# GpSimd's weight sums of two gate chunks, held behind two results of VectorE

## What is computed

```python
h = rms_norm(x); proj = h @ w_in            # q/k/v of both branches, beta, decay, gates
y_a = diff_attention(dq, dk, dv)            # 4 heads, two softmaxes each: p0 - lam*p1
y_b = gated_delta_net(...) * silu(g_gate)   # 4 chunks of 64 tokens, solved by inverses
merged = sigmoid(m_gate_a) * (y_a @ w_branch_attn) + sigmoid(m_gate_b) * (y_b @ w_branch_gdn)
x = x + merged @ w_out
x = x + hier_moe(rms_norm(x))               # 32 experts, top 2 of one group
return rms_norm(x)
```

## Time and profile before

| | us |
|---|---|
| median of 3 runs | 458.78 (458.12 to 460.59) |
| the profiled execution, its own time | 460.23 |
| its span, first to last instruction | 458.5 |
| PE busy | 427.2 (93%) |
| DVE busy | 223.8 (49%) |
| ACT busy | 124.3 (27%) |
| POOL busy | 60.2 (13%), 94 instructions |
| mean granted clock of PE | 0.970 |
| moved by DMA | 136.92 MB, 299 GB/s on average |

### The profile page before, as it was taken

How to read it: one execution, slowest core, us unless ns; L and a number is a source line. 1 busy time by engine, 2 the same in 40 slices (tenths; PEclk the granted TensorE clock), 3 DMA queues, 4 the chain that set the end, 5 groups by cost and what they waited for, 6 DMA issues and landing times.

```text
span 458.5 us, 10749 instructions
## 1 busy us (share of the span) xinstructions
PE 427.2 (93%) x4503; PEld 340.8 (74%) x4503; DVE 223.8 (49%) x573; ACT 124.3 (27%) x326; POOL 60.2 (13%) x94
## 2 busy tenths in 40 slices
PE   8999999999997999999999899999999987779784
PEld 7885598884896999988888778677686755537451
DVE  3376777996366388513322655343444522432233
ACT  5001522100500163610012533233242312222144
POOL 4010600000693449000000000000000000000001
PEclk9999999999997999999999999999999988998798
DMA  8969726325704053298996999999999999999992
GB/s 306 410 231 326 268 80 221 101 86 151 264 10 175 1 184 124 68 400 338 414 415 260 325 409 425 416 419 422 422 422 421 420 422 422 420 422 422 422 380 101
DMA packets 38197, 136.92 MB, mean 299 GB/s; under 512 B 8592, under 2 KB 9936, under 8 KB 26256
## 3 DMA queue, kind: packets, MB, share of 16 engines
q1 hardware_dynamic: 33808, 135.22, 74.7%
q10 hardware_dynamic: 4352, 1.21, 1.2%
HBM read 134.59 MB, written 1.84 MB: 298 GB/s over the span
## 4 chain that ended last, share of the span: by engine, by line
PE 74%; DMA 18%; DVE 3%; SPq 1%; ACT 1%; issue 1%; POOLq 0%; ACTq 0%; DVEq 0%
PE ps L996 21%; DMA arena<-in_moe_w_up 11%; PE ps L1447 10%; PE ps L1042 10%; PE ps L1311 6%; PE ps L1295 6%; DMA ring<-in_moe_w_up 6%; PE ps L1500 3%; PE ps L1490 3%; PE ps L1406 2%; PE ps L1455 1%; PE ps L1057 1%; SPq L437 1%; DMA cst_in<-in_norm_ffn_gain 1%; PE ps L1395 1%
## 5 line engine op out<-in xcount | busy, mean ns | idle before, releaser
L996 PE MATMUL ps<-arena 128*128 128x256 f32 (+1 forms) x384 | 98.6, 416 | 0.0
L996 PEld LDWEIGHTS ps<-arena 128*128 128x128 f32 x384 | 72.2, 190 | 22.3 <-issue 14.2
L1447 PE MATMUL ps<-arena 128*32 128x128 f32 x1040 | 40.5, 296 | 9.5 <-DMA arena<-in_moe_w_up 8.9
L1447 PEld LDWEIGHTS ps<-arena 128*32 128x32 f32 x1040 | 31.3, 115 | 16.1 <-DMA arena<-in_moe_w_up 7.7
L793 ACT ACTIVATE gains<-ps 32x256 f32<-32x256 f32 x62 | 23.3, 377 | 55.9 <-PE ps L1490 55.5
L559 POOL TENSOR_SCALAR ring<-ring,small 128x512 f32<-128x512 f32 x1 | 1.6, 1567 | 268.1 <-DVE small L2148 268.1
L2194 DVE TENSOR_TENSOR masks<-ps,masks 128x64 f32<-128x64 f32 x32 | 7.2, 224 | 54.8 <-ACT masks L774 54.6
L542 POOL TENSOR_TENSOR ring<-arena 128x256 f32<-128x256 f32 x32 | 22.9, 748 | 82.0 <-DMA arena<-in_w_in 70.8
L2210 DVE COPY arena<-ps 32x256 f32<-32x256 f32 x62 | 25.8, 416 | 11.2 <-PE ps L1490 10.2
L1447 PE MATMUL ps<-ring,arena 128*32 128x128 f32 x768 | 26.9, 278 | 3.6 <-DMA ring<-in_moe_w_up 3.4
L1311 PE MATMUL ps<-arena 128*128 128x256 f32 x128 | 29.3, 383 | 0.0
(11 more groups left out here) (323 smaller groups left out, 596.4 us busy)
## 6 DMA issues: line engine op xcount, KB each, us to landing
arena<-in_moe_w_down SPq DMA_DIRECT2D x19, 1024.0 KB, 26.4
arena<-in_w_in SPq DMA_DIRECT2D x8, 2048.0 KB, 8.5
arena<-in_moe_w_gate SPq DMA_DIRECT2D x16, 1024.0 KB, 22.4
arena<-in_moe_w_up SPq DMA_DIRECT2D x16, 1024.0 KB, 23.6
ring<-in_moe_w_gate SPq DMA_DIRECT2D x12, 1024.0 KB, 19.6
ring<-in_moe_w_up SPq DMA_DIRECT2D x12, 1024.0 KB, 20.5
ring<-in_moe_w_down SPq DMA_DIRECT2D x12, 1024.0 KB, 21.6
arena<-in_w_out SPq DMA_DIRECT2D x2, 2048.0 KB, 10.3
```

The source lines that it names most:

```text
L996: last = pe.matmul(out, lhs, rhs, start=(k == 0 and (i > 0 or part % 2 == 0)), stop=(k == KD - 1), skip_group_check=(i == 0))
L1447: last = pe.matmul(c.ps[ROWS * q:ROWS * (q + 1), i % 2, 0:P], c.Hg[:, k, ROWS * i:ROWS * (i + 1)], w[:, :, start:start + 127:2], start=(k ...
```

## The change

Two waits are added to GpSimd's program. In chunk `ma1` it waits for `aT_in` (the first call of `combine` done) before the first of the four forms, so all sixteen sums come behind it. In chunk `mb1` it waits for `yb_ready` before the third form, so the last eight sums (S4 and S3) come behind it. Nothing else changes: no instruction is added to another engine and none is moved within its engine.

```diff
         free("P5")
+        if name == "ma1":
+            pool.wait_ge(s["aT_in"], 1)
         combine("S1", w["A21"], w["A22"], ALU.add)
         pool.wait_ge(s["forms_combined"], combined(name, "S1"))
         free("P6")
         combine("S2", form["S1"], w["A11"], ALU.subtract)
         pool.wait_ge(s["forms_combined"], combined(name, "S2"))
         free("P3")
+        if name == "mb1":
+            pool.wait_ge(s["yb_ready"], 1)
         combine("S4", w["A12"], form["S2"], ALU.subtract)
         free("P7")
         combine("S3", w["A11"], w["A21"], ALU.subtract)
```

## The result

| | before | changed |
|---|---|---|
| median of 4 runs, us | 458.54 (458.12 to 460.59) | 454.18 (452.95 to 454.64) |
| profiled execution, its own time | 460.23 | 452.95 |
| its span | 458.5 | 451.2 |
| mean granted clock of PE | 0.970 | 0.983 |

The ratio is 0.9891 with a 95% interval of 0.9862 to 0.992: 4.4 us less by the medians, 7.3 us less between the two profiled executions. The forecast was 452.7, in a range of 451.2 to 455.8.

What follows compares the result with a forecast made beforehand. TensorE bounds the stretch from 110 to 230 us, weights the experts. Terms: -3.35 (wait) - 3.04 (clock) + 0.3 (L1910) = -6.1 us, giving 454.1 against the profiled 460.23, 452.7 against the median; range 451.2 to 455.8.

Steps and rivals of the forecast that it cites:

- the first rival: Clock falls anyway in the stretch behind the first turning, so only the wait is saved: 455.7 us; chance 5%.
- What bounds the kernel, and how a gain carries: Weights pace the experts; TensorE sets the stream's start, so its gain before 240 us moves the end by as much.
- The sums slow `combine`: GpSimd's sums in `ma1` slow VectorE's first `combine`; without them it ends at 137.34, not 141.45.
- The wait goes, 3.35 us: PE's wait before L1199, the first probabilities' transposes, vanishes; start moves from 141.60 to 138.25, a gain of 3.35 us.
- The clock, 3.04 us: From L1199 to L1208, PE's clock stays at 1.00: 4.04 us in place of 7.08, a gain of 3.04.
- bounds of 5.8 and 6.5 us: The gain's own limits: 5.8 with L1910 at 0.52 and TensorE's last matmul drained at 138.4; 6.5 with L1910 free.
- The 0.3 us at L1248: A PE wait before L1248, released by ScalarE; expected to be 0.3 to 0.9 us in the changed trace.
- L1910, 0.3 us: VectorE's small scaling ending the second query block's maxima may meet a sum: cost 0 to 0.52 us, taken as 0.3.
- Second hold, nothing: The hold in `mb1` saves 3 us of VectorE's time at L2042's eight multiplies, none of the kernel's.
- Second right sides beside sums: VectorE's `second_right_sides` (L1966), newly beside sums, costs 0 to 1.9 us extra, hidden by over 2 us of slack.
- That sums don't matter: Rival: another cause makes `combine` long, or the hold doesn't keep sums out; no gain, 458.8 to 459.1 us; chance 4%.
- GpSimd as the bound: Rival: delayed sums make TensorE wait at P6 and P7 of `ma1`, clock falling again for 3.0: 461.4 us; chance 3%.

Runs made afterwards that it cites:

- e1: The changed kernel with only the hold in `ma1`, none in `mb1`: 454.63 us, ratio 0.9903 to the kernel before.
- e4: The changed kernel plus 16 sums without use ahead of the hold in `ma1`, beside the first `combine`: 459.38 us, ratio 1.0005 to the kernel before.
- e7: The kernel before plus 13 matmuls without use ahead of the first turning of probabilities: 457.93 us, ratio 0.9961 to the kernel before.
- e3: The kernel before plus 27 matmuls without use ahead of the first turning of probabilities: 460.46 us, ratio 1.003 to the kernel before.
- after_again: The changed kernel run once more, unaltered, for a narrower interval and a second trace: 454.87 us, ratio 0.991 to the kernel before.
- e2: The changed kernel with only the hold in `mb1`, none in `ma1`: 459.91 us, ratio 1.0016 to the kernel before.
- e5: The changed kernel plus 14 memsets without use ahead of the hold in `ma1`: 456.39 us, ratio 0.9939 to the kernel before.
- e6: The changed kernel plus 8 sums without use behind the hold in `ma1`, ahead of the real ones: 458.01 us, ratio 0.9968 to the kernel before.

## Why the prediction was right, and where its size was off

The mechanism was right in both of its parts, and the forecast gain of 6.1 us was too large by a quarter or more. That the median still fell into the range is in part luck. The lower end of the gain was set by the first rival, a clock that falls in any case, and not by a stall that varies, and the median of 454.18 lies as far from the forecast (452.7) as from that rival (455.7). The number alone doesn't tell the two apart; the traces do.

**What bounds the kernel, and how a gain carries: right.** The weight stream moved with TensorE: 6.4 us at L1212 (6.9 with what lay before the mark) and 6.7 at the stream's last loads.

**The sums slow `combine`: right, shown** by e1 (with the first hold, whole gain) and e4 (idle sums in the same place, no gain). The end of `combine` was worked out as 137.34. The four scalings took 0.87 against a bound of 1.14, so it came at 136.7, on a trace that began 0.5 us earlier. At L1212 the trace read gives 6.4 us, which is 3.35 + 3.04 with nothing paid at L1910.

**The wait goes, 3.35 us: right for the trace read, too large on average.** Its row is one draw: five traces with sums beside `combine` had 3.19, 2.05, 3.15, 1.97 and 3.20 us, a mean of 2.7 (2.6 with the 2.01 of e4).

**The clock, 3.04 us: this term was mis-sized.** The mechanism holds, as the fill of e7 shows: idle time ahead, the clock falls; none, it stays. But the prediction took one execution's loss for the kernel's. Measured from the turning to L1208, over the 4.0 us at full clock, the loss was 3.1 us in the trace of before, 0.6, 3.0 and 2.2 in the three extra ones and 1.7 with only the second hold, a mean of 2.1; the 0.3 us wait at L1229 is within the 0.6 and the 2.2. The fill of e7 gained 1.5 to 1.8, with the fill's own cost taken off. The stretch as a whole gave 31.38 - 26.40 = 5.0 us on average (4.6 with the trace of e4 as a sixth). e3 gives the same by another way: its fill outlasts the stall whether that is 2.0 or 3.2 us, so from mark to L1211 it takes 148.27 - 115.85 = 32.42 us, and its median lay 1.0 above the kernel before, which puts that at 31.4 by this estimate. The prediction had noted that the profiled execution lay 1.45 us above the median and still moved the full 6.1 us over to the median. A stall that varies is likely to be above its mean in a slow execution; 6.1 less 1.45 would have been 4.7, a sum that is easy to make afterwards. It isn't the whole of the scatter, though: of the three extra traces the one with the least loss was the fastest (457.26 us), but the middle one was as slow (460.25) as the largest (460.14). The medians differ by 4.4, 4.6 and 4.8 us (the last with the first hold alone). The interval of after_again reaches from 2.9 to 5.4 us, so these runs can't tell them from 5.0. The falls of the clock in the routing, which both traces of the changed kernel have and the four of the kernel before don't, are not the change's doing alone: e2 and e7, without the first hold, have them (a mean clock of 0.93 and 0.91 from 240 to 260 us), and e1, with it, doesn't. What they cost stays open.

**Small slips in its sums.** The prediction's bounds of 5.8 and 6.5 us come out at 5.7 (3.2 + 3.04 - 0.52) and 6.4 (3.35 + 3.04). The 0.3 us at L1248 is a wait of the weight loads, not of PE, whose only wait there was the 3.2 us.

**L1910, 0.3 us: not paid, but the danger was real.** The sums of `mb0` ended at 153.74 and L1914 started at 153.60, yet took 0.17. Three runs pushed the sums later: in e5 and e6 it took 0.70 and 0.71, and PE stood 0.7 us behind it; in e4 its two instructions took 0.19 and 0.56, and PE stood 0.2 us. The term's upper bound, 0.52, was right (0.71 - 0.17 = 0.54). In the changed kernel the two rows even overlap by 0.14 us, and GpSimd's spans are rough, so by how much the place is clear isn't shown.

**Second hold, nothing: right** (e2: 1.0016, interval 0.9997 to 1.0035). **Second right sides beside sums: right,** 1.12 us with sums beside them (L1970), the lower bound.

**The rivals.** That the clock falls anyway: refuted, 1.00 from 138 to 150 us in all five traces with the first hold and nothing beside `combine`. That sums don't matter: refuted by e4. GpSimd as the bound: not reached, since a sum stayed at 0.70 us beside VectorE's readers of PSUM. e6 shows what it would have been had the sums come later: waits at P5 and P6 of `ma1`, where the rival named P6 and P7, and no fall of the clock behind them, which the rival had priced at 3.0.

## What to carry to other kernels

Where VectorE has a short chain with all operands in SBUF on the critical path, look for what GpSimd does beside it: an instruction of VectorE that lasts as long as one of GpSimd's is the sign, and a semaphore that holds GpSimd back until the chain is done costs nothing as long as GpSimd's own readers have slack. Work the slack out in both directions; here 5.5 us more delay would have eaten two thirds of the gain. And a stall of a few microseconds, with its clock loss, is one draw from several values: cost it from several traces, or take the full figure of one trace for the upper end.

## What was not expected of the hardware

The clock's answer to a stall of the same place and length varies between executions of one program: with about 2.0 us of standing it stayed at 1.00 in two traces (the first extra one of before, and e4) and fell in one, and with 3.2 us it cost 3.1, 3.0 and 1.7 us. The length of the stall itself had two values, 2.0 and 3.2 us, by whether VectorE's first scalings slipped in ahead of a sum. And where the critical chain had no such collision, the stretch was the same, 26.39 or 26.40 us, in all five traces.
